# Fourteen modulation blocks moved from TensorE rows at scattered places to running sums on VectorE inside the first feed-forward block

## The reference

```python
c_act = jax.nn.silu(c)
mod = c_act @ mod_w[i] + mod_b[i]
sh_m, sc_m, gt_m, sh_f, sc_f, gt_f = jnp.split(mod, 6, axis=-1)
h = rmsnorm(x, norm_pre_mix[i]) * (1.0 + sc_m) + sh_m
y = conformer_conv_module(h, ...)
x = x + gt_m * rmsnorm(y, norm_post_mix[i])
h = rmsnorm(x, norm_pre_ffn[i]) * (1.0 + sc_f) + sh_f
y = conv_ffn(h, ...)
x = x + gt_f * rmsnorm(y, norm_post_ffn[i])
...
ada = jax.nn.silu(c) @ w_ada + b_ada
sh1, sc1, g1, sh2, sc2, g2 = jnp.split(ada, 6, axis=-1)
ada_c = jax.nn.silu(c_ctx) @ w_ada + b_ada
```

## Time and profile before

| what | us |
|---|---|
| median of 3 runs | 3415.69 (3413.41 to 3417.14) |
| the profiled execution, time | 3414.27 |
| its span | 3412.5 |
| TensorE busy | 3188.2 (93%) |
| VectorE busy | 1561.4 (46%) |
| ScalarE busy | 1017.6 (30%) |
| GpSimd busy | 440.7 (13%) |
| granted TensorE clock, mean | 0.963 of full |

### The profile page before, as it was taken

How to read it: one execution, slowest core, us unless ns; L and a number is a source line. 1 busy time by engine, 2 the same in 40 slices (tenths; PEclk the granted TensorE clock), 3 DMA queues, 4 the chain that set the end, 5 groups by cost and what they waited for, 6 DMA issues and landing times.

```text
span 3412.5 us, 33468 instructions
## 1 busy us (share of the span) xinstructions
PE 3188.2 (93%) x13802; PEld 2481.6 (73%) x13802; DVE 1561.4 (46%) x1706; ACT 1017.6 (30%) x1217; POOL 440.7 (13%) x183
## 2 busy tenths in 40 slices
PE   6897889999999999989999998899989999999996
PEld 1683556668888888768888876676666788888885
DVE  4677655563343443574411155576335522222225
ACT  3344435333222222233221132476223221111111
POOL 0497660000000000000200043000010000000002
PEclk8998998899999999999999999999998999999998
DMA  5113453312111211331332333621432122111112
GB/s 199 44 44 129 164 172 109 99 66 64 62 37 50 62 31 44 118 111 60 138 111 99 123 132 115 148 64 47 154 106 93 71 65 62 38 50 62 31 50 105
DMA packets 96191, 301.23 MB, mean 88 GB/s; under 512 B 11205, under 2 KB 15045, under 8 KB 95847
## 3 DMA queue, kind: packets, MB, share of 16 engines
q1 hardware_dynamic: 96040, 299.09, 27.0%
HBM read 251.34 MB, written 47.71 MB: 88 GB/s over the span
## 4 chain that ended last, share of the span: by engine, by line
PE 46%; DVE 5%; ACT 2%; DMA 1%; issue 1%; POOL 0%; SPq 0%; DVEq 0%
PE ps L675 38%; PE ps L1076 2%; PE ps L1101 1%; PE ps L721 1%; PE ps L736 1%; PE ps L826 1%; PE ps L1086 1%; DMA mainr<-sc_k 1%; DVE tmp L2238 1%; DVE tmp L2232 1%; DVE tmp L2234 1%; ACT mainr L1557 0%; POOL tmp L2457 0%; DVE cols L2288 0%; PE ps L776 0%
## 5 line engine op out<-in xcount | busy, mean ns | idle before, releaser
L675 PE MATMUL ps<-mainr,wh 128*128 128x512 f32 (+1 forms) x7104 | 1937.2, 390 | 39.9 <-POOL wl L2397 11.9
L675 PEld LDWEIGHTS ps<-mainr,wh 128*128 128x128 f32 x7104 | 1334.2, 189 | 319.3 <-issue 43.5
L675 PE MATMUL ps<-mainr,wl 128*128 128x512 f32 (+1 forms) x3552 | 1129.7, 389 | 0.0
L675 PEld LDWEIGHTS ps<-mainr,wl 128*128 128x128 f32 x3552 | 671.1, 189 | 138.3
L1688 DVE TENSOR_TENSOR wl<-raw,wh 128x1024 fp32r<-128x1024 f32 (+2 forms) x256 | 255.0, 998 | 549.5 <-ACT wh L1200 549.4
L1200 ACT CAST wh<-raw 128x1024 fp32r<-128x1024 f32 (+2 forms) x320 | 281.4, 885 | 711.2 <-PE ps L675 579.8
L736 PE MATMUL ps<-raw,cols 128*1 128x512 f32 (+1 forms) x384 | 191.2, 650 | 44.3 <-DVE mainr L2010 18.2
L2397 POOL TENSOR_TENSOR wl<-raw,wh 128x1024 fp32r<-128x1024 f32 x64 | 154.3, 2418 | 451.5 <-ACT wh L1200 451.5
L1921 DVE TENSOR_TENSOR mainf<-mainf,ps 128x1024 f32<-128x1024 f32 x80 | 97.6, 1220 | 221.1 <-PE ps L675 220.7
L2442 POOL TENSOR_TENSOR tmp<-tmp,mainf 128x1024 f32<-128x1024 f32 x8 | 27.5, 3436 | 1196.5 <-DVE tmp L2208 1196.5
L1960 DVE SCALAR_TENSOR_TENSOR ps<-mainf,vec,ps 128x1024 f32<-128x1024 f32 (+1 forms) x174 | 181.0, 1103 | 0.8 <-ACT ps L1393 0.7
(11 more groups left out here) (228 smaller groups left out, 2600.6 us busy)
## 6 DMA issues: line engine op xcount, KB each, us to landing
raw<-in_mod_w SPq DMA_DIRECT2D x48, 512.0 KB, 4.5
raw<-in_ada_w SPq DMA_DIRECT2D x48, 512.0 KB, 3.8
raw<-in_f_up SPq DMA_DIRECT2D x44, 512.0 KB, 3.4
raw<-in_g_up SPq DMA_DIRECT2D x44, 512.0 KB, 3.5
raw<-in_w_in SPq DMA_DIRECT2D x40, 512.0 KB, 4.0
raw<-in_pw SPq DMA_DIRECT2D x24, 512.0 KB, 3.5
sc_x<-mainf SPq DMA_DIRECT2D x24, 512.0 KB, 3.6
mainf<-sc_x SPq DMA_DIRECT2D x24, 512.0 KB, 6.3
```

The costliest lines, as they stand in the source:

```text
L675: ins = e.matmul(out, wt[:, a:b], xs[n], start=kk == 0 and t == 0, stop=kk == kt - 1 and t == 2)
```

## The change

Fourteen of the 24 blocks (m10, m11, a0 to a11) are no longer multiplied on TensorE. Their raw weights enter the ring within feed-forward "f", marked "sum": two per up tile at (1,0) to (2,1) and (11,0) to (18,1), one per up tile (blocks with two rows) at (3,0) to (10,1). For each, VectorE does four instructions of 128x512: accumulator = weight x column + accumulator, in `S(0)` or `S(1)`. After the last raw weight of a block, TensorE sums over partitions with 128x1 matmuls (`modulation_columns`, four per row: 72 matmuls for the 14 blocks), behind the next up tile (i, 0), and VectorE adds the bias (`modulation_sum_add`).

The other ten stay as they were, six of them now after filter steps 3, 5, 7, 19, 21 and 23; GpSimd's and VectorE's loops do the taps of the two steps left out in four other steps (`DOUBLE`). The block ends run without modulation and take the first three tiles with the plain `tiles_abreast`; the first columns of the products with the stream move from the block end to just before the last k-step of the last tile of the projection. At most two split weights are prepared ahead. Line numbers move by 14 to 34: L736 becomes L771, L675 L710, L1200 L1214, L1308 L1318, L1325 L1335.

```diff
+def summed_modulations():
+    parts = [("m", jb, kp) for jb in (10, 11) for kp in range(4)] + [("a", jb, kp) for jb in range(12) for kp in range(4)]
+    out, at = {}, (1, 0)
+    while parts:
+        n = 1 if parts[0][0] == "a" and parts[0][1] < 4 else 2
+        out[at], parts = parts[:n], parts[n:]
+        at = (at[0], 1) if at[1] == 0 else (at[0] + 1, 0)
+    return out
...
-    mods = iter([("m", j) for j in range(4, 12)] + [("a", 0)])
+    mods = iter([("m", j) for j in range(4, 10)])
...
-        if s % 16 < 8 and s % 2 == 1:
+        if s % 16 < 8 and s % 2 == 1 and s not in (1, 17):
...
+DOUBLE = (9, 11, 13, 15)
...
     def block_end(s, x, ready):
...
+        last_squares(s)
         residual(s)
-        modulation("a", mods[0], (2, 3))
         norm_spread(n)
-        for step in range(8):
-            part(0, step)
...
+        tiles_abreast(keys, 8, x, ready)
...
-        tile((s, ND - 1), 8, x, ready, lambda: summed_squares(s))
+        tile((s, ND - 1), 8, x, ready, lambda: (summed_squares(s), products_with_stream(s)))
+
+    def modulation_columns(kind, jb):
+        hold_aux("dmc", kind, jb, banks=(0,))
+        w.wait_ge(*k.at(*k.sum_last(kind, jb)))
+        src, rows = k.S(jb % 2), summed_rows(kind, jb)
+        for c in range(4 * rows):
+            ins = e.matmul(ps[:, 3072 + c:3073 + c], src[:, 128 * c:128 * c + 128], m.ones[:, 0:1], start=c == 0,
+                           stop=c == 4 * rows - 1)
...
-            if i == 0:
-                modulation_row("a", mods[0])
-            if i == 4:
-                modulation_row("a", mods[1])
-        split_to(k.W[keys[2]] + 10)
+        split_to(k.W[keys[2]] + 2)
...
+    def modulation_part(j):
...
+        for r in range(rows):
+            acc = k.S(jb % 2)[:, 512 * r:512 * r + 512]
+            for n in range(2):
...
+                if kk == 0:
...
+                    e.tensor_scalar(acc, src, c, None, ALU.mult).then_inc(*k.to("dmp", j, r, n))
+                    continue
...
+                e.scalar_tensor_tensor(out=acc, in0=src, scalar=c, in1=acc, op0=ALU.mult, op1=ALU.add).then_inc(*k.to("dmp", j, r, n))
...
-    modulation("a", 1)
-    modulation("a", 2)
     sum_columns("ln")
...
-        if QT <= n < QT + 3:
-            modulation("a", 7 + n - QT)
-            if n > QT:
-                modulation_turn("a", 6 + n - QT)
-    modulation_turn("a", 9)
```

More of the change, by code:

```diff
@@ L58, with summed_at, summed_rows @@
 LAST = len(CHUNKS) - 1
-NEXT = {"pw2": ("n2", (3, 4), (("f_up", 0, 0), ("f_up", 0, 1), ("f_up", 1, 0))),
-        "f": ("n3", (5, 6), (("w_in", 0), ("w_in", 1), ("w_in", 2))),
-        "w_out": ("n4", (10, 11), (("g_up", 0, 0), ("g_up", 0, 1), ("g_up", 1, 0)))}
+NEXT = {"pw2": ("n2", (("f_up", 0, 0), ("f_up", 0, 1), ("f_up", 1, 0))),
+        "f": ("n3", (("w_in", 0), ("w_in", 1), ("w_in", 2))),
+        "w_out": ("n4", (("g_up", 0, 0), ("g_up", 0, 1), ("g_up", 1, 0)))}
+def summed_modulations():
[6 more added lines that the diff above has]
+    return out
+SUMMED = summed_modulations()
+def summed_at(i):
+    return [(kind, jb) for n in range(2) for kind, jb, kp in SUMMED.get((i, n), ()) if kp == 3]
+def summed_rows(kind, jb):
+    return 2 if kind == "a" and jb < 4 else 1
 def u_at(i):
@@ L433, in residual_plan @@
             return
-        n, mods, first = NEXT[s]
+        n, first = NEXT[s]
         self.tmp.only(*range(NTMP))
@@ L490, in ffn_plan @@
                         self.tmp.take(("cv", i, n), *([("ulo", s, i)] if n else [("um", s, i)]))
+                        for kind, jb, kp in SUMMED.get((i, n), ()):
+                            self.weight((kind, jb, kp), self.d["mod_w" if kind == "m" else "ada_w"][4 * jb + kp], 1024, "sum")
                     else:
                         self.acc.take((s + "_up", i, n), *([("um", s, i)] if n else [("us", s, i)]))
+                if s == "f" and i:
+                    for what in summed_at(i - 1):
+                        self.aux[0].take(("dmc", *what), ("mod", *what, summed_rows(*what) - 1))
                 if s == "g":
@@ L809, in block_end @@
     def block_end(s, x, ready):
[L812 to L831 removed]
+        n, keys = NEXT[s]
+        last_squares(s)
         residual(s)
[L833 removed]
         norm_spread(n)
[L835 to L848 removed]
+        tiles_abreast(keys, 8, x, ready)
     def sum_columns(s):
@@ L877, in ffn @@
                         tile((s + "_up", step[1], n), 8, x, ready)
+                    if s == "f" and n == 0 and step[1]:
+                        for what in summed_at(step[1] - 1):
+                            modulation_columns(*what)
             else:
@@ L1429, in scalar_program @@
             filter_step(s)
-            products(1)
+            products(2 if s in DOUBLE else 1)
         else:
@@ L1701, in modulation_add, with modulation_sum_add @@
             e.tensor_tensor(k.COL(name, 4 * jb, 4), cols[:, r, :], k.V(base, 4 * jb, 4), ALU.add).then_inc(*k.to("mod", kind, jb, r))
+    def modulation_sum_add(kind, jb):
+        w.wait_ge(*k.at("dmc", kind, jb))
+        for r in range(summed_rows(kind, jb)):
+            name, base = (("mod", "modb"), ("ada" if r == 0 else "adac", "adab"))[kind == "a"]
+            e.scalar_tensor_tensor(out=k.COL(name, 4 * jb, 4), in0=m.ps[:, 3072 + 4 * r:3076 + 4 * r], scalar=1024.0,
+                                   in1=k.V(base, 4 * jb, 4), op0=ALU.mult, op1=ALU.add).then_inc(*k.to("mod", kind, jb, r))
     def modulation_weights(kind, jb, ahead):
@@ L1891, in ffn @@
                                                op0=ALU.mult, op1=ALU.add).then_inc(*k.to("cv", i, n))
+                    for what in summed_at(i - 1):
+                        modulation_sum_add(*what)
                     src = k.TMP("cv", i, 1)
@@ L2096, in vector_program @@
             row = (kind, s)
-    modulation_add(*row)
     conv_steps(turns, 1000)
-    for jb in (1, 2):
-        modulation_weights("a", jb, 1)
     w.wait_ge(*k.at("mean"))
@@ L2507, in residual @@
         if s in NEXT:
-            first = k.W[NEXT[s][2][2]] + 9
-            feed(first)
+            feed(k.W[NEXT[s][1][2]] + 1 + RAW)
         for i in range(ND):
@@ L2513, in residual @@
             e.dma_start(d[key][i], x(i)).then_inc(*k.land(f"st{i}", key))
-            if s in NEXT and 1 <= i <= 4:
-                feed(first + i)
     def again(i, dst, key):
@@ L2584, in sync_program @@
             feed_modulation(kind, s)
-    feed_modulation("a", 1)
-    feed_modulation("a", 2)
+    feed(k.W["pw2", 0] + 1)
     w.wait_ge(*k.at("tile", k.W["filt", 1, 3, 1]))
@@ L2693, in sync_program @@
         head_values(0, half)
-    feed(k.W["a", 7, 3] + 1)
+    feed(k.W["hy_up", 3])
     for hd in range(1, NH):
```

131 lines of the change are left out of this document (50 added, 81 removed).

## The result

The changed kernel takes 3382.6 us, the median of 4 runs (3380.13 to 3385.08), against 3415.55 for the kernel before: a ratio of 0.9904 (95% interval 0.9887 to 0.9921). A second set on another occasion gave 0.9899 (0.9885 to 0.9912). The forecast was 3382.

What follows compares the result with a forecast made beforehand. The prediction took TensorE to bound the kernel in feed-forward "f" and VectorE's path to bound the block ends. Its terms summed to -33.3 us, giving a forecast of 3382 us, with an 8-in-10 range of 3367 to 3404.

Steps and rivals of the forecast that it cites:

- convolution stage: First stage: one row block less in each half, 4.7 and 5.6 us, plus a slow row loop's 1.7; -12.1 us.
- the end of attention: Start of `hy_up` tile 0, freed from three row loops and a queued load: -20.8, cold restart +1.8, -19.0 us together.
- the five gaps that the change opened at stage ends: Five places losing row matmuls as fillers; one TensorE restart at half clock priced at 1.8 us in each.
- The late mean: End of the convolution stage: the mean's matmuls start right behind VectorE's sum instead of behind block a0, -10.4 us.
- The wait ahead of f_up (1, 1): After `pw2`'s block end: the tile's weight cast stands behind the first pair's chain and two sums, so it starts +3.6 us.
- Columns: Feed-forward "f": 72 matmuls of 128x1, 144 records, all on TensorE's path, +17.0 us (bounds 10 and 20).
- The block ends of "f" and `w_out`: Two bias adds leave each; "f" -2.0 us with a cold restart, `w_out` -9.1 us with its next tile sooner.
- the chain over ScalarE's casts: End of attention: Hyena product casts start up to 7 us earlier, then weight casts and lower parts; `hy_up` starts near 2391.3.
- A: Rival: all matmuls of three block ends and two other places run at 1.2 GHz; about +15 us, 3397; chance 0.2.
- B: Rival: the clock holds, restarts cost nothing and f_up (1, 1) comes as before; 12.6 us less, 3369; chance 0.14.
- C: Rival: VectorE or the load ring cannot follow in "f"; +36 to +72 us, say 3430; chance 0.08.
- D: Rival, chance 0.13: end of attention and convolution stage give only -6 each; 3401. In "mean to D": a block-end event.

Runs made afterwards that it cites:

- the doubled sums: Changed kernel with every VectorE sum instruction issued twice in a row; f_up (1, 1) to the last dn tiles took 672.6 us, against 673.3 in the changed kernel.

## Why the forecast came true, and where it didn't

**The total was right partly because errors cancelled.** The convolution stage was 6 to 9 us short of its term, "f" 2 us worse than forecast; the end of attention (4 to 4.6 better), the stretches from the mean to D (2.5 to 3.7 better together) and the last stretch (0.8 to 1.5) made it good. That 3382 met 3382.6 this closely is luck.

**The step that failed** is "Convolution stage: -12.1". It priced a block by what VectorE idles at it (4.7 and 5.6) and took the one slow row loop (8.72) to leave with the block. The slow loops stayed: 9.07 at 295.72 and 8.79 at 323.59 in the changed kernel. Nor is the row of 8.72 the only slow one of that half in the kernel before: the loop at 284.25 takes 8.99. And the filter steps left without a loop ran at half speed, 3.78 for 1.85. There are four of them, so they add 7.7 us, against the 6.1 to 8.7 by which the term was too large. (The term's own parts, 4.7, 5.6 and 1.7, add up to 12.0.) I had weighed the clock in the five gaps that the change opened at stage ends, and not here, where the loops were seen as cost alone. Putting the rows back showed 3.1 to 6.6 us.

**Terms that held.** The late mean, -10.4 as forecast. The wait ahead of f_up (1, 1), +3.8 for +3.6, and by the mechanism named. Columns, 16.9 for 17.0; the trace sided with its row of 106 ns a record. The issue floor of about 25 ns that the Trainium skill gives ("TensorE: Matmul & The Clock Gate", section "Back-to-back issue gap"), by which it would have been 3.6, is a lower bound, and this case stays well above it. The stretch over "f" came out at +20.7: 16.9 for the columns, 2.2 for the restart at 711.93 (two tiles take 23.9, until 735.84, where 21.8 is usual) and 1.6 for a fall of the clock behind a wait of 2.54 (755.81); the kernel before has that wait too (766.46), without the fall. VectorE's load in a pair: 15.1 of 22 over two pairs instead of 16.0. The 13.9 of the window shown is low because it has all eight sums but cuts off part of the pair's own work. The block ends of "f" and `w_out`: -1.8 and -9.8 for -2.0 and -9.1 in the first pair of profiles, but -3.0 and -6.4 in the second, so they hold only to some 3 us.

**The end of attention** gave 23.0, not 19.0. The cold restart of 1.8 that I added isn't there: TensorE went from the last products straight into the tile. The other 2.2 are the chain over ScalarE's casts, which I took for what is late next. It is not on the path: the weight's cast was done before attention, the first cast of the Hyena product ends at 2392.2, and TensorE's own last products hold the tile until 2394.26. That is 10.0 behind the last head's spread, and in the kernel before it is 33.2. The reason that I gave for the gain, row loops and a queued load, was incomplete: the row matmuls are 9.4 of it, and the larger part is what goes with them.

**The rivals.** A (the clock takes more back) was right in its mechanism, though not in its time: the clock of the block end fell from 0.87 to 0.77 and filling the gaps won some 3 us in each end, where the forecast had put 1.8 on the clock in an end and A 4 to 5. The rule of the Trainium skill cited beside the forecast ("TensorE: Matmul & The Clock Gate", section "HAM oscillation — how this bites in real kernels") agrees with this case behind the long waits: after 10.00 and after 4.02 four matmuls take 2.05 for 1.07. B is excluded, f_up (1, 1) came late and cold. C is excluded by the doubled sums. D was half right: in the convolution stage the gain did fall short, though not because of GpSimd: in both profiles of the changed kernel no wait of another engine in the stage is ended by GpSimd, which waits for ScalarE itself.

The 0.8 to 1.5 us that the end of "g" gained are no gain of the change, as far as the traces go. TensorE's tiles of "g" keep the same pace in both kernels, and the difference arises at the last sixteen column records, which take 3.57 in the kernel before (3380.05) and 1.95 and 3.02 in the changed kernel's two profiles (3352.48 and 3349.01): a clock that fell or not.

What stays open is why the clock is up or down at one and the same code: there, and in the stretch before the mean, which takes 221 or 225 us.
